# Scan inverse as two diagonal 64x64 parts with one block product between them, unread products in the waits of its levels, and the first expert's gather from unscaled rows

## The reference

```python
def _wkv7_step(state, inp):
    r, w, k, v, a, b = inp
    sa = jnp.einsum('phvk,phk->phv', state, a)
    state = state * w[:, :, None, :] + sa[..., None] * b[:, :, None, :] + v[..., None] * k[:, :, None, :]
    return state, jnp.einsum('phvk,phk->phv', state, r)
...
    x = _layer_norm(alpha * x + mix, ln1_g, ln1_b)
    logits = (xf @ router_w).astype(jnp.float32) + router_b
    top_v, top_i = lax.top_k(logits, TOP_K)
    gate = jax.nn.softmax(top_v, axis=-1)
    # every chosen expert e: ((u + 1) * (g * sigmoid(g * 1.702))) @ w2[e] + b2[e], with [g, u] = x @ w1[e] + b1[e]
```

## Time and profile before

| | us |
|---|---|
| median of 3 runs | 1201.5 (1199.6 to 1202.71) |
| the profiled execution | 1201.52 |
| its span | 1199.7 |
| PE busy | 1146.6 (96%) |
| DVE busy | 287.6 (24%) |
| ACT busy | 216.5 (18%) |
| POOL busy | 32.7 (3%) |
| DMA moved | 430.69 MB, mean 359 GB/s |

### The profile page before, as it was taken

The page is one execution under the profiler, slowest core; times in us unless marked ns, Lnnn a source line. Parts: engine busy times, 40 slices in busy tenths (PEclk is TensorE's granted clock), DMA queues, the critical chain, the costliest instruction groups (busy, mean ns, idle before and its releaser), DMA issues.

```text
span 1199.7 us, 14540 instructions
## 1 busy us (share of the span) xinstructions
PE 1146.6 (96%) x5836; PEld 502.8 (42%) x5836; DVE 287.6 (24%) x742; ACT 216.5 (18%) x453; POOL 32.7 (3%) x67
## 2 busy tenths in 40 slices
PE   7999999999999999999999999999999999999996
PEld 6875878753333333333333333333333333333332
DVE  1368566662111111111111111111111111111113
ACT  1345554411111111111111111111111111111112
POOL 1000122100000000000000000000000000000001
PEclk9999999999999999999999999999999999999999
DMA  8525202289999999999999999999999999999994
GB/s 333 203 106 202 99 1 77 107 327 367 406 428 428 428 428 429 429 428 428 428 428 428 429 380 428 428 428 429 428 429 428 428 428 428 428 428 428 428 422 191
DMA packets 34586, 430.69 MB, mean 359 GB/s; under 512 B 3857, under 2 KB 4017, under 8 KB 8449
## 3 DMA queue, kind: packets, MB, share of 16 engines
q1 hardware_dynamic: 33296, 427.15, 84.9%
q0 software_dynamic: 544, 2.06, 0.5%
q10 hardware_dynamic: 720, 1.15, 0.3%
HBM read 429.29 MB, written 1.05 MB: 359 GB/s over the span
## 4 chain that ended last, share of the span: by engine, by line
PE 60%; DMA 32%; DVE 5%; ACT 1%; issue 1%; SPq 1%; POOL 0%; POOLq 0%; DVEq 0%
PE bank L1398 19%; DMA pool<-in_exp_w 17%; DMA ring<-in_exp_w 15%; PE bank L1434 14%; PE bank L981 5%; PE bank L991 3%; PE bank L1370 2%; PE bank L1280 2%; PE bank L1380 2%; PE bank L1418 1%; DVE pool L2005 1%; DVE pool L2000 1%; DVE pool L2002 1%; PE bank L1151 1%; PE bank L1166 1%
## 5 line engine op out<-in xcount | busy, mean ns | idle before, releaser
L1434 PE MATMUL bank<-ring,pool 128*64 128x512 f32 x1024 | 228.4, 596 | 9.4 <-DMA ring<-in_exp_w 9.4
L1398 PE MATMUL bank<-ring,pool 128*64 128x512 f32 x1024 | 228.0, 595 | 6.5 <-DMA ring<-in_exp_w 6.4
L1398 PE MATMUL bank<-pool 128*64 128x512 f32 x1024 | 228.0, 595 | 5.7 <-DMA pool<-in_exp_w 5.3
L1434 PEld LDWEIGHTS bank<-ring,pool 128*64 128x64 f32 x1024 | 70.0, 137 | 165.9 <-issue 145.0
L1398 PEld LDWEIGHTS bank<-ring,pool 128*64 128x64 f32 x1024 | 71.2, 137 | 158.7 <-issue 142.8
L1398 PEld LDWEIGHTS bank<-pool 128*64 128x64 f32 x1024 | 71.3, 137 | 157.7 <-issue 144.1
L1986 DVE TENSOR_SCALAR pool<-pool 128x128 f32<-128x128 f32 x64 | 19.4, 346 | 428.6 <-PE bank L1398 428.6
L921 ACT ACTIVATE pool<-pool 128x512 f32<-128x512 f32 x32 | 20.2, 632 | 472.2 <-DVE pool L1998 472.2
L1998 DVE TENSOR_SCALAR pool<-bank 128x512 f32<-128x512 f32 x32 | 22.2, 693 | 316.8 <-PE bank L1398 316.8
L981 PE MATMUL bank<-pool,ring 128*128 128x256 f32 x272 | 61.2, 387 | 7.1 <-DMA ring<-in_w_in_C 7.1
L931 ACT ACTIVATE pool<-bank 128x512 f32<-128x512 f32 x32 | 19.2, 599 | 258.0 <-PE bank L1434 258.0
(11 more groups left out here) (300 smaller groups left out, 858.2 us busy)
## 6 DMA issues: line engine op xcount, KB each, us to landing
ring<-in_exp_w SPq DMA_DIRECT2D x126, 2048.0 KB, 22.7
pool<-in_exp_w SPq DMA_DIRECT2D x63, 2048.0 KB, 27.0
ring<-in_w_out SPq DMA_DIRECT2D x2, 2048.0 KB, 7.7
ring<-in_exp_w SPq DMA_DIRECT2D x4, 1024.0 KB, 14.5
ring<-in_w_in_A SPq DMA_DIRECT2D x1, 2048.0 KB, 13.5
ring<-in_w_in_B SPq DMA_DIRECT2D x1, 2048.0 KB, 7.9
ring<-in_w_in_D SPq DMA_DIRECT2D x1, 2048.0 KB, 13.6
ring<-in_w_in_H SPq DMA_DIRECT2D x1, 2048.0 KB, 7.8
```

What stands on the lines that cost most here:

```text
L1398: last = mm(bank[4 + g][hp, :], lhs, w[:, k % 2, o:o + 512], start=False, stop=(k == KD - 1))
L1434: last = mm(bank[6][SLOTS * hf:SLOTS * hf + SLOTS, :], hT[:, k % 4, SLOTS * (k // 4):SLOTS * (k // 4) + SLOTS], w2s[k // 4][:, k % 4, 512 ...
```

## The change

The 128x128 inverse is now built only to two diagonal 64x64 parts in levels 1 to 5, with both parts side by side in one 128x64 tile (`y_blocks`, 256 columns for four blocks where it was 512). Level 6 works out the block between them (`last_level`, from `m_last`, which ACT copies out of the raw products), and `u` takes two products for each block. `neighbours` becomes products with the folding matrix `C_FOLD`. `keep_busy` issues products into PSUM columns that nothing reads: in `gate_cols`, twice in level 1, and at the end of levels 1 to 5; a narrower one stands in levels 1 and 5. The two turns of `bt` and `kt` move from level 2 to level 1. The identities are laid before the last gelu, and PE no longer waits for that gelu before the first products. At the router's end the first gather reads the centred, unscaled rows `grp`; the scale is in `sel`, and the LayerNorm bias comes from a product with `ones`. `scaled(1)` moves behind `sel` and behind the number of passes on DVE; the residual of the second half goes from PE to ACT; the residual of the first half is split. SP's load of the odd slot 2 and POOL's load of `lnr` wait for the gather as well. The diff, cut to its core:

```diff
-        c[:, o + 2 * P:o + 3 * P] = before.T
+        c[:, o + 2 * P:o + 3 * P] = before.T & (row // HD == col // HD)
...
+    c[:, C_FOLD:C_FOLD + HD] = row[:, 0:1] % HD == np.arange(HD)[None, :]
...
-        m_early = [view(o_xT + 512 * b, 2, 2, P) for b in range(4)]
+        m_early = [view(o_xT + 512 * b, 2, 2, P) for b in range(3)]
+        m_last = view(o_xT + 1536, 2, 4 * HD)
         ym = rview(3, 0, 2, 4, P)
         oT = rview(3, 3584, NCH, P)
-        tT = rview(3, 1024, 2, 2, P)
+        tT = rview(3, 1024, 2, P)
...
             sp.wait_ge(s_x1, NCH)
+            sp.wait_ge(s_gath, 1)
             load_slot(1, 2, True)
...
+            act.wait_ge(s_ops, NP - 1)
+            identities()
             gelu(5)
...
-                if n < NL - 1:
-                    A(by_late(ym[:, d], d, n + 1), split(y, d, n + 1), ACT.Copy).then_inc(s_xup, 1)
+                if n < NL - 2:
+                    A(by_late(y_blocks(d), n + 1), split(y_bank(d), d, n + 1), ACT.Copy).then_inc(s_xup, 1)
+                elif n == NL - 2:
+                    A(y_blocks(d), bank[4 * d + 1][:, 0:4 * HD], ACT.Copy).then_inc(s_xup, 1)
                 else:
-                    A(ym[:, d], y, ACT.Copy).then_inc(s_xup, 1)
...
+                    first = rows_of(d)
+                    A(y_last(d)[first], pview(4 * d + 1, 4 * HD, 4, HD)[first], ACT.Copy).then_inc(s_xup, 1)
...
+                            later, first = rows_of(1 - d), rows_of(d)
+                            for h in (1, 0):
+                                act.wait_ge(s_prev, 4 * pt + 2 * d + 2 - h)
+                                A(m_last[later, d].rearrange("p (j s) -> p j s", j=4)[:, 2 * h:2 * h + 2],
+                                  pview(4 * d + h, 0, 2, 2, P)[later, :, 1, first], ACT.Copy).then_inc(s_ml, 1)
                             turned_in(pt, 0, d)
                     for d in range(2):
                         act.wait_ge(s_tt, 12 * pt + 2 * n + d - 1)
-                        A(tT[:, d], pview(4 * d + 2, 0, 2, P), ACT.Copy).then_inc(s_tev, 1)
+                        A(tT[:, d], bank[4 * d + 2][:, 0:P], ACT.Copy).then_inc(s_tev, 1)
...
+                    if n == NL - 1:
+                        for d in range(2):
+                            later = rows_of(1 - d)
+                            A(y_last(d)[later], y_bank(d)[later], ACT.Copy).then_inc(s_yl, 1)
...
+            def residual():
+                act.wait_ge(s_x1e, 4)
+                act.wait_ge(s_x1, 2)
+                for hf in range(2):
+                    last = A(bank[2 + hf][:, :], x_tok[:, 1, 512 * hf:512 * hf + 512], ACT.Copy, scale=ALPHA)
+                return last
...
+            def keep_busy(out):
+                n = out.shape[1]
+                mm(out, ident, kst[:, 0:n], start=True, stop=True, skip_group_check=True)
             def gate_cols():
+                keep_busy(bank[7][:, 0:256])
...
-            pe.wait_ge(s_base, NT + 6)
+            pe.wait_ge(s_base, NT + 5)
...
+                    pe.wait_ge(s_ml, 4 * pt + 2 * d + 1)
                     for j in range(4):
-                        last = mm(pview(4 * d + 1, 0, 4, P)[:, j], ym[:, d, j], ident, is_transpose=True, start=(j == 0),
-                                  stop=False, skip_group_check=True)
+                        last = mm(y_bank(d)[:, j], ym[:, d, j], scan_const(C_FOLD, HD), start=(j == 0), stop=False,
+                                  skip_group_check=True)
...
+                def level(n, d):
+                    pe.wait_ge(s_me, 10 * pt + 2 * n + d - 1)
+                    if n == 1:
+                        pe.wait_ge(s_ml, 4 * pt + 2 * d + 2)
+                    tr(bank[4 * d + 2][:, 0:P], y_early(d), ident).then_inc(s_tt, 1)
+                    for b in range(2):
+                        last = mm(pview(4 * d, 0, 2, P)[:, b], m_early[(n - 1) % 3][:, d, b], y_late(d), start=True, stop=True)
+                    last.then_inc(s_a, 1)
+                def last_level(d):
+                    first, later = rows_of(d), rows_of(1 - d)
                     for jj in range(2):
-                        last = mm(pview(4 * d, 0, 2, P)[:, jj], m_early[(n - 1) % 4][:, d, jj],
-                                  y_late(d)[:, 2 * jj:2 * jj + 2], start=True, stop=True)
+                        last = tr(bank[4 * d + 2][:, HD * jj:HD * jj + HD], y_blocks(d)[first, P * jj:P * jj + P],
+                                  ident[first, first])
+                    last.then_inc(s_tt, 1)
...
                     pe.wait_ge(s_tev, 12 * pt + 2 * n + d - 1)
-                    for jj in range(2):
-                        last = mm(part(pview(4 * d + 1, 2 * P * jj, 2, P), n, 1 - d), tT[:, d, jj], gm[:, d, jj],
-                                  start=False, stop=(n == NL - 1), skip_group_check=True)
+                    if n < NL - 1:
+                        for b in range(2):
+                            bp = rows_of(b)
+                            last = mm(part(y_bank(d)[bp], n, 1 - d), tT[:, d, bp], gm[:, d, b], start=False, stop=False,
+                                      skip_group_check=True)
+                    else:
+                        for jj in range(2):
+                            o = 4 * HD + P * jj
+                            last = mm(bank[4 * d + 1][rows_of(d), o:o + P], tT[:, d, HD * jj:HD * jj + HD], gm[:, d, jj],
+                                      start=(jj == 0), stop=True, skip_group_check=True)
...
+                        if n == 1:
                             tr(pview(4 * d + 2, 0, 4, P)[:, 2], bt[:, d, d], ident)
                             tr(pview(4 * d + 2, 0, 4, P)[:, 3], kt[:, d, d], ident).then_inc(s_bk, 1)
...
+                        if n == 1:
+                            pe.wait_ge(s_ml, 4 * pt + 2 * d + 2)
+                            keep_busy(bank[4 * d][:, 0:256])
                         pe.wait_ge(s_xup, 2 * NL * pt + 2 * (n - 1) + d + 1)
-                        turn_early(n, d)
-                        cross(n, d)
+                        if n < NL - 1:
+                            level(n, d)
+                        else:
+                            last_level(d)
...
+                    if n == 1 or n == 5:
+                        mm(bank[1][:, 4 * HD:6 * HD], ident, kst[:, 0:P], start=False, stop=False, skip_group_check=True)
...
+                    if n < NL - 1:
+                        keep_busy(bank[0][:, 256:512])
...
                         for h in range(2):
                             j = 2 * h + c
-                            last = mm(pview(4 * d + 2, 256, 4, HD)[:, j], ym[:, d, j], wbuf[:, d, j], start=True, stop=True)
+                            u = pview(4 * d + 2, 256, 4, HD)[:, j]
+                            mm(u[first], y_block(d, j)[first], wbuf[first, d, j], start=True, stop=True)
+                            last = mm(u[later], y_last(d)[:, j], wbuf[:, d, j], start=True, stop=True)
...
+            def residual(hf):
+                pe.wait_ge(s_x1, 1)
+                mm(bank[hf][:, :], al_id, x_tok[:, 0, 512 * hf:512 * hf + 512], start=True, stop=False, skip_group_check=True)
...
+            pe.wait_ge(s_al, 1)
+            residual(1)
...
+            residual(0)
...
+            def gather_rows(rows, first):
                 for c in range(NCH):
                     for hf in range(2):
-                        last = mm(bank[7][SLOTS * hf:SLOTS * hf + SLOTS, :], sel[:, c], x_tok[:, c, 512 * hf:512 * hf + 512],
-                                  start=(c == 0), stop=(c == NCH - 1))
...
+            for hf in range(2):
+                mm(bank[7][SLOTS * hf:SLOTS * hf + SLOTS, :], ones[0:1, 0:SLOTS], lnr[0:1, 1, 512 * hf:512 * hf + 512],
+                   start=True, stop=False, skip_group_check=True)
             pe.wait_ge(s_sel, 1)
+            gather_rows(grp, False)
+            pe.wait_ge(s_bias, 48)
+            pe.wait_ge(s_esel, 1)
+            pe.wait_ge(s_moe, 2)
+            bias_rows((0,))
+            gather_turn(1)
+            bias_rows((1,)).then_inc(s_esu, 1)
+            pe.wait_ge(s_zero, 2)
             pe.wait_ge(s_x1, NCH)
-            gather_rows()
-            residual(1)
...
+                if n > 3:
+                    pool.wait_ge(s_a, 12 * pt + 2 * (n - 3))
...
+                    for b in range(2):
+                        cols = mp[:, d, 1, :, rows_of(b)].rearrange("p j (b two m) -> p two j b m", two=2, m=LEVELS[n])[:, d]
+                        last = nc.gpsimd.tensor_copy(m[:, b].rearrange("p (j b m) -> p j b m", j=4, m=LEVELS[n]), cols)
+                    last.then_inc(s_me, 1)
...
+            pool.wait_ge(s_gath, 1)
             pool.dma_start(lnr, ln_rows[:, 2:4]).then_inc(s_late2, 16)
...
-                    for h in range(2):
+                    for h in (1, 0):
...
-                        last = V.tensor_scalar(sel[:, c], iota[:, 0:SLOTS], posm[:, c, 0:1], None, ALU.is_equal)
```

(41 more changed lines are left out.)

70 lines of the change are left out of this document (30 added, 40 removed).

## The result

| | before | after |
|---|---|---|
| median | 1200.85 us (1199.6 to 1202.71, 16 runs) | 1205.75 us (1202.24 to 1217.02, 16 runs) |
| the profiled execution, its span | 1201.52, 1199.7 | 1209.12, 1207.3 |
| mean granted clock of single runs | 0.997 in the profiled one | 0.983 to 0.997 |

The ratio is 1.0049 [1.0037, 1.0062]: 4.9 us slower, where 4.1 us faster was forecast. Two things are to be seen: the fastest runs differ by 2.6 us only, and the runs after spread over 15 us instead of 3. The time follows the granted clock: 1202.24 at 0.997, 1205.89 at 0.993, 1209.91 at 0.990, 1217.02 at 0.983. So there are a fixed part and a part that varies.

What follows compares the result with a forecast made beforehand. The experts were taken as a fixed-length load stream released by the first expert's start, so savings ahead of it shorten the whole. Later passes +0.4, first pass -2.8, router -1.7 gave -4.1 us: 1197.4 us, range 1191.5 to 1201.5.

Steps and rivals of the forecast that it cites:

- Level 6 and the tail: End of each later scan pass: instruction counts stay except `u`, 0.9 to 1.0 us instead of 0.9; together +0.1 us.
- The direction at 126 us: First pass, level 3: with fillers the clock drop at 126 to 130 us goes, level 3 takes 3.15 us, -1.1.
- The third rival: The clock drops all the same: first pass level 3 keeps 4.28 us, a later stretch costs +1.0; 1199.5 us, chance 0.15.
- the forecast's -4.4: The forecast change of the whole kernel, in us, without its +0.3 for `u`.
- The -1.7: Router's end: the first expert starts at 276.3 us, 1.7 us earlier, bounds -0.8 and -2.2.
- half of the bias rows (0.5): Router's end: half of the bias rows takes 0.5 us on PE, beside ACT's copy (0.6).
- The fourth rival: Loads swallow the router's gain: the load at 275.0 and `lnr` close the stream 1.5 us late; 1199 us, chance 0.1.
- start: Start of each later scan pass: longer `neighbours`, moved turns and fillers make level 2 late by +1.2 us.
- levels 1 to 5: Later pass: start with level 1 +1.2 us, level 2 +0.2, level 3 -0.35, level 4 -0.75, level 5 -0.2.
- The first pass: First scan pass: earlier start -1.0 us, level 2 +0.15, level 3 -1.1, the rest -0.85; sum -2.8, bounds -4.5 and -0.5.
- The slower rival: PE becomes the bound of all levels through fillers and folds, +2.3 us a pass, +4.6 in all; 1206 us, chance 0.1.
- the 0.53 us each that stood in the sum: Scan passes: one `keep_busy`, a product with 256 moving columns in two instructions, priced at 0.53 us on PE.

Runs made afterwards that it cites:

- e1: The changed kernel with both `u` products on all 128 rows, ACT clearing the rows of `y_blocks` that must not count: 1194.14 us, ratio 0.9940.
- e3: The kernel before with only each `u` product split as in the change, into one 64x64 and one 128x64 product: 1207.54 us, ratio 1.0053.
- e6: The kernel before with each `u` product written as two of 64 weight columns, both on all 128 rows: 1199.45 us, ratio 0.9990.
- e2: The changed kernel with `u` reordered: for each stage and direction first the two 64x64 products, then the two 128x64 ones: 1202.25 us, ratio 1.0019.
- e5: The changed kernel with `u` products on all 128 rows and without any of its idle filler products: 1204.32 us, ratio 1.0028.
- e8: The changed kernel with `u` on all 128 rows, keeping only fillers at the scan's entry and ahead of level 1: 1208.62 us, ratio 1.0047.
- e11: The changed kernel with `u` products on all 128 rows, run again on the chip of e8, e9 and e10: 1196.94 us, ratio 0.9965.
- e9: The changed kernel with `u` on all 128 rows, keeping only fillers behind the updates and the narrow ones: 1195.79 us, ratio 0.9967.
- e10: The changed kernel with `u` on all 128 rows, without the filler behind the update of level 5: 1201.17 us, ratio 0.9987.

## Why the prediction was wrong

**The step that failed** is in "Level 6 and the tail": "`u` is 16 instructions with 64 weight columns instead of 8 with 128: 0.9 to 1.0 instead of 0.9." It measured 2.06 and 2.07, for the stage comes twice a pass: +6.6 us in all where +0.3 stood. The price was taken from rows of 128x64 tiles of one shape, and for these it was right, even too high (e1: 0.40 us for 16). What had no row in the trace of before was the alternation of 64x64 and 128x64, and I gave it the price of the nearest row and no upper bound. The bound to take was one in which nothing overlaps between neighbours. The Trainium skill (TensorEngine Tiling (Array Packing), Key Properties) has the rule that speaks against this change: switching the tiling mode drains the engine. The traces agree, in e3 against e6 and in e2 against after: a product of two instructions costs 0.257 us in the mix and 0.05 in one shape (e1, first stage). That rule was not weighed among the rivals.

**The clock** was the second error. The direction at 126 us was right (1.00 in the window after), yet the account took fillers as a cost with one drop to remove. They are a need: without them the new levels ran at 0.972 to 0.989 (e5, e8). With them it is only just enough: the runs of e1 and its repeats on three chips went from 0.989 to 0.998. After's median lies 3.5 us above its fastest run, that of before 1.25. The third rival had this ("one stretch of thinner levels in a later pass drops too") but at 1.0 us; one long drop costs 5.5. The split alone does not do it (e3, median 0.8 us above the fastest run). The thin levels alone can: of e1's three sets, two have medians within 0.9 us of the fastest run, but the third, e11, lies 3.6 us above it, as much as after. Whether the mixed shapes make it worse is not shown: on one chip e2 had four of ten runs above 1208 us and e1 no such run in six, which are few, and after's 15 us of spread against e11's 9 may be a difference between chips. What exactly starts a drop stays open; the place differs from run to run.

The totals close: fastest runs +2.6 = -4.0 + 6.6; medians +4.9 = 2.6 + 3.5 - 1.25. That -4.0 lies so near to the forecast's -4.4 is in part luck. Level 6 was sized at nothing and gave 2.6 us; the router gave 0.65 less than forecast, and the rest behind the first expert was 1.1 us longer in the profile after than in that before.

**The router.** The -1.7 was -1.05 with the clock up. The term that was mis-sized is "half of the bias rows (0.5)". Chain of waits, before and then after:

```profile
277.07 1.02 PE bank L1380 x8
```

```profile
281.86 1.00 PE bank L1462 x4
...
283.54 1.01 PE bank L1462 x4
```

Eight instructions over two groups of 32 rows took 1.02 us; four over one group take 1.00. By these times the two groups ran side by side, so to split them doubled their time: the turn waits 0.25 us longer than forecast and the expert 0.4 more, the 0.65 that is missing. The fourth rival, that late loads swallow the gain, finds no support: its 1.5 us do not show in the medians of the rest (920.8 and 920.9). What takes the gain back in six of the twelve profiled executions is a drop of the clock in the gather.

**Right:** start +1.15 for +1.2, and levels 1 to 5, whose sum is +0.15 for +0.1. The first pass, 40.72 to 39.7 us, is -1.0, or -3.2 without the two `u` stages, for -2.8 forecast, but 0.9 of it is level 6. The slower rival named 1206, and the time fell there, but by another mechanism: PE did not become the bound of levels by fillers (level 5 is 2.80, below 2.87). e9's fastest run against e11's makes the seven fillers at the entry and ahead of level 1 cost 0.9 us in all, a fraction of the 0.53 us each that stood in the sum; that most of it lies in waits is my reading. e10's makes the three behind level 5 cost 0.7, near the 0.3 each of the sum.

**The best version** is e1: medians 1194.14, 1196.94 and 1193.71 on three chips, ratios 0.9940, 0.9965 and 0.9945, about 6 us faster than before and, by the medians, 9 to 12 faster than after.

## What to carry to other kernels

Count the changes of shape on PE, not only the instructions: a product cut to the rows it needs can cost far more than one that runs over zeros, if its neighbour has another shape (here sixteen instructions took 2.06 us instead of 0.40). Keep one shape in a run; in e1 and e6 it was fast on alternate column halves.

Where an edit makes PE's work thinner, ask what holds the clock afterwards, and read several runs' clocks beside their times: a median that lies far above the fastest run is a clock problem, and one profile may not show it.

An operation that no row shows needs an upper bound from what serialises it.

## What the runs showed of the hardware

- Sixteen fp32 instructions of 64 weight and 64 moving columns on alternate column halves of 128 rows take 0.40 to 0.43 us; on shapes that change after every two, 2.06. With four of one shape on one column half between the changes it is 1.51 (e2), 0.37 to 0.39 for each four. How much of that is the change and how much staying on one half is not shown.
- Four bias products on one group of 32 rows take as long as eight on two groups, 1.00 and 1.02 us.
- Ratios of e1 differ by 0.25% between chips (0.9940 on one, 0.9965 on another), and its runs' clocks with them (0.994 to 0.998, and 0.989 to 0.998), while the fastest runs agree within 0.1 us (1193.3, 1193.37, 1193.3).
